# Row blocks of the normed x and the split weights at other addresses modulo 128

## What is computed

```
x = layer_norm(x, ln_emb_g, ln_emb_b)
h = x @ w_in + b_in                          # 1024 x 1992
...
x = layer_norm(DN_ALPHA * x + mix, ln1_g, ln1_b)
q = x @ xa_wq + bq
...
f = square(relu(x @ w_up + b_up)) @ w_down + b_down    # 1024 x 4096 and back
...
```

## Time and profile before

| what | value |
|---|---|
| median of three runs | 1988.37 us |
| the profiled execution's own time | 1989.87 us |
| its span, first to last instruction | 1988.1 us |
| granted TensorE clock, mean | 0.959 |
| TensorE (PE) busy | 1802.6 us, 91% |
| VectorE (DVE), ScalarE (ACT), GpSimd (POOL) busy | 967.8, 783.5 and 621.1 us |

### The profile page before, as it was taken

How to read it: one execution, slowest core, us unless ns; L and a number is a source line. 1 busy time by engine, 2 the same in 40 slices (tenths; PEclk the granted TensorE clock), 3 DMA queues, 4 the chain that set the end, 5 groups by cost and what they waited for, 6 DMA issues and landing times.

```text
span 1988.1 us, 22738 instructions
## 1 busy us (share of the span) xinstructions
PE 1802.6 (91%) x8994; PEld 1421.1 (71%) x8994; DVE 967.8 (49%) x1871; ACT 783.5 (39%) x1329; POOL 621.1 (31%) x223
## 2 busy tenths in 40 slices
PE   7895778989899999998988999999999899999998
PEld 6673554787788888887766777877787667676776
DVE  5167887444543121225646653455553544435355
ACT  4452453253264132313444444344445343433333
POOL 2332145121223434451233433443412132121320
PEclk9897889989999999998988999999999999999999
DMA  7212010121112222321111112221112111111101
GB/s 270 95 64 85 22 43 24 40 86 43 62 66 106 89 103 85 106 96 43 67 62 50 56 64 74 75 80 49 64 65 77 43 44 66 55 54 64 65 22 43
DMA packets 27409, 137.51 MB, mean 69 GB/s; under 512 B 2815, under 2 KB 9215, under 8 KB 13480
## 3 DMA queue, kind: packets, MB, share of 16 engines
q1 hardware_dynamic: 26248, 135.02, 19.2%
q10 hardware_dynamic: 1056, 1.05, 0.2%
HBM read 133.93 MB, written 2.12 MB: 68 GB/s over the span
## 4 chain that ended last, share of the span: by engine, by line
PE 68%; DVE 15%; ACT 9%; issue 4%; POOL 2%; DMA 1%; SPq 0%; DVEq 0%; ACTq 0%; POOLq 0%
PE ps L1166 67%; ACT whi L1564 2%; PE ps L1170 2%; POOL wlo L2502 1%; DVE STT L2414 1%; DVE XL L1996 1%; DVE tmp L2166 1%; DVE R L1996 1%; DVE mx L1999 1%; DVE SCB L2226 1%; ACT LG L1565 1%; DVE m L2224 1%; ACT tmp L1564 1%; ACT PM L1565 1%; ACT BH L1564 1%
## 5 line engine op out<-in xcount | busy, mean ns | idle before, releaser
L2502 POOL TENSOR_TENSOR wlo<-raw,whi 128x2048 fp32r<-128x2048 f32 (+3 forms) x123 | 527.2, 4286 | 1135.1 <-ACT whi L1564 1135.1
L1166 PE MATMUL ps<-XH,whi 128*128 128x512 f32 (+1 forms) x1144 | 447.8, 391 | 10.0 <-DVE XL L1996 4.7
L1166 PE MATMUL ps<-XH,wlo 128*128 128x512 f32 (+1 forms) x1144 | 425.9, 372 | 0.0
L1166 PE MATMUL ps<-XL,whi 128*128 128x512 f32 (+1 forms) x1144 | 425.9, 372 | 0.0
L1564 ACT ACTIVATE whi<-raw 128x2048 fp32r<-128x2048 f32 (+3 forms) x129 | 230.5, 1787 | 160.7 <-PE ps L1166 158.1
L1166 PEld LDWEIGHTS ps<-XH,whi 128*128 128x128 f32 x1144 | 221.6, 194 | 63.8 <-issue 20.0
L1166 PEld LDWEIGHTS ps<-XL,whi 128*128 128x128 f32 x1144 | 222.1, 194 | 36.5 <-issue 2.2
L1166 PEld LDWEIGHTS ps<-XH,wlo 128*128 128x128 f32 x1144 | 221.3, 193 | 37.5
L1166 PE MATMUL ps<-BH,whi 128*128 128x512 f32 (+1 forms) x608 | 229.1, 377 | 3.9 <-DVE BL L2436 2.0
L2096 DVE TENSOR_TENSOR R<-ps,R 128x512 f32<-128x512 f32 (+1 forms) x164 | 94.0, 573 | 270.3 <-PE ps L1166 269.9
L1166 PE MATMUL ps<-BH,wlo 128*128 128x512 f32 (+1 forms) x608 | 218.2, 359 | 0.0
(11 more groups left out here) (296 smaller groups left out, 2911.7 us busy)
## 6 DMA issues: line engine op xcount, KB each, us to landing
raw<-wall SPq DMA_DIRECT2D x108, 1024.0 KB, 4.6
raw<-wall SPq DMA_DIRECT2D x9, 512.0 KB, 3.3
raw<-wall SPq DMA_DIRECT2D x8, 576.0 KB, 3.4
raw<-wall SPq DMA_DIRECT2D x4, 768.0 KB, 4.0
R<-xT SPq DMA_DIRECT2D x1, 2048.0 KB, 13.9
BFL<-scr SPq DMA_DIRECT2D x16, 128.0 KB, 3.3
outT<-R SPq DMA_DIRECT2D x16, 128.0 KB, 1.9
MEM<-memT SPq DMA_DIRECT2D x2, 512.0 KB, 4.5
```

The source lines that it names most:

```text
L1166: return nc.tensor.matmul(o_, l, r_, start=start, stop=stop, skip_group_check=True)
L2502: tt(wlo[u % NSPL][:, 0:n], raw[u % NRAW][:, 0:n], f32(whi[u % NSPL][:, 0:n]), ALU.subtract).then_inc(S("g_lo"), 1)
```

## The change

It moves tiles; it adds and removes no instruction, and every engine has the same instructions, waits and order as before (12,626 instructions in both programs).

- The scratch for dynamic transfers at the bottom of each partition shrinks from 16384 to 128 bytes, and the counter starts at 512 and not at 16512. Both are multiples of 128.
- `whi0`, `wlo0`, `whi1`, `wlo1` now lie in this order with 32 bytes behind each: they start at 0, 32, 64 and 96 modulo 128.
- A row block of `XH` and `XL` now takes 516 elements (2064 bytes), of which 512 are used: row block k starts at 16 k modulo 128, in both tiles alike. `XL` starts 16512 bytes behind `XH`, again a multiple of 128.
- All other tiles keep their remainder modulo 128.

```diff
-        base = 16512
+        base = 512
...
         raw = [sb(f"raw{i}", [128, UNIT]) for i in range(NRAW)]
-        whi = [sb(f"whi{i}", [128, UNIT], F32R) for i in range(NSPL)]
-        wlo = [sb(f"wlo{i}", [128, UNIT], F32R) for i in range(NSPL)]
+        whi, wlo = [], []
+        for i in range(NSPL):
+            whi.append(sb(f"whi{i}", [128, UNIT], F32R))
+            top[0] += 32
+            wlo.append(sb(f"wlo{i}", [128, UNIT], F32R))
+            top[0] += 32
+        top[0] = (top[0] + 127) // 128 * 128
         x_at = top[0]
-        XH = sb("XH", [128, 8, T], F32R)
-        XL = sb("XL", [128, 8, T], F32R)
+        XH = sb("XH", [128, 8, T + 4], F32R)
+        XL = sb("XL", [128, 8, T + 4], F32R)
+        top[0] = (top[0] + 127) // 128 * 128
...
-                    return XH[:, k, :], XL[:, k, :]
+                    return XH[:, k, 0:T], XL[:, k, 0:T]
...
-    nc = _bacc.Bacc("TRN2", target_bir_lowering=False, num_devices=1)
+    nc = _bacc.Bacc("TRN2", target_bir_lowering=False, num_devices=1, dynamic_dma_scratch_size=128)
```

## The result

The changed kernel takes 1998.70 us (median of six runs, 1993.71 to 2003.88) against 1988.12 us before (six runs, 1987.53 to 1989.78): a ratio of 1.0052, with a 95% interval of 1.0031 to 1.0073. It is slower by half a per cent. Its six times fall in two groups of three, near 1993.8 and near 2003.7 us, so the median lies between them, where no execution is; the profiled execution, 2003.88 us, is of the upper one. The kernel before shows nothing like it in these six, but it does in later ones (see "The two groups of times").

A forecast was written before the change was run, and what follows sets the result against it. TensorE, busy 91% of the span, was taken as the bound through the spacing of its split matmuls. The terms summed to +5.7 us, nine tenths of it +5.1, so 1988.4 became 1993.5 us; 8-in-10 range 1972 to 2006.

The forecast's parts named there:

- a change of that spacing goes nearly straight into the time: Split matmuls on TensorE hardly wait, so their start spacing sets the time; nine tenths of a change reaches the end.
- the long stretch: 1344 matmuls in 306.40 us without TensorE idling; forecast about 308.7 us, under 303 if faster, over 312 if far slower.
- X, 512: 2664 matmuls on XH and XL, 512 columns: mean distance to the weights becomes the middle, 3.3 ns each, +8.8 us.
- B, 512: 1248 matmuls on BH and BL, 512 columns: even units +1.1 ns, odd units +5.5 ns, together +4.1 us.
- B2 and QC, 512: 600 matmuls on B2H, B2L, QCH, QCL, 512 columns: leave distance 64 for a mixture, -3.3 ns each, -2.0 us.
- X and B, 256: 1344 matmuls with 256 columns: spacing falls by half the gap between 120.1 and 113.4 ns, -4.5 us.
- B2, 256: 192 matmuls on B2H and B2L, 256 columns: spacing rises by 3.35 ns each, +0.6 us.
- a straight line between the two: Unread distances modulo 128 between 0 and 64 get interpolated spacings, 3.3 ns at distance 32; a choice, not a reading.
- B by unit: Sign: B's 512-column spacing should alternate, near 227.8 ns in even units and 232.2 ns in odd units.
- Nothing to measure: Rival: spacing settles near the old value or gains cancel losses; 1984.4 to 1992.4 us, chance 0.26.
- Faster: Rival: XH/XL 512-column matmuls drop 6.7 ns to 220 ns, 1972.4 us; with B, 1964.8 us; chance 0.30.
- Slower by far: Rival: settled pattern lost because starts shift with each row block; XH/XL, BH/BL at 233.3 ns, 2012.0 us, chance 0.10.

The follow-up runs named there:

- The kernels of constant distances: Kernel before with small scratch and counter at 512, weights or X, B, B2 moved to other fixed starts, no stagger: 1993.90, 1995.67, 2003.70 and 2000.78 us.

## Why the prediction was right, and where it was off

**The direction and the mechanism held.** The step "a change of that spacing goes nearly straight into the time" is borne out: the stretch without idle grew by 5.0 us and nothing hides it. The small scratch at 0 us was right, and GpSimd nearly so: TensorE waited 1.4 us longer at `wlo` before its largest group. The granted clock in the long stretch stayed at 1.00, as forecast.

The prediction also weighed the Trainium skill, page "TensorE: Matmul & The Clock Gate", section "Step-by-step: what each phase is for", by which the two read ports are independent and loading the next weights takes no read bandwidth from the running matmul. The reading put on it, that an address would then change nothing, is refuted: moving the weights alone took X from 226.7 to 232.3 ns. Whether that happens at the ports no run here shows.

**The size.** I forecast +5.1 us on the median; it is +10.6, just over twice that. How near that is to the sum below is in part luck, since the median lies between two groups: the lower is +5.7 us from the median before, the upper +15.7, and the ten later executions of the same kernel have a median of +7.6. That the lower group lies near the forecast is luck as well: its matmuls are spaced as in the upper, and its profiles lose 5 us less at the lower clock than that of the kernel before (table above). The spacings are the firmer measure. Averages over all steps at full clock that follow one another directly, before to after, against the terms of the sum:

| term | per matmul forecast | measured | us forecast | us measured |
|---|---|---|---|---|
| X, 512 | +3.3 ns | 227.9 to 231.6, +3.7 | +8.8 | +9.8 |
| B, 512 | +3.3 | 227.9 to 232.5, +4.6 | +4.1 | +5.8 |
| B2 and QC, 512 | -3.3 | 233.3 to 232.2, -1.1 | -2.0 | -0.7 |
| X and B, 256 | -3.3 | 119.7 to 117.8, -1.9 | -4.5 | -2.5 |
| B2, 256 | +3.35 | 114.8 to 117.8, +3.0 | +0.6 | +0.6 |

With the memory's keys (192 matmuls, -0.4; the 192 of the values are left out) the sum is +12.6 instead of +5.7. The step that was mis-sized is the choice "a straight line between the two" and, under it, the distance modulo 128. The line took every unread distance for the middle between a good and a bad reading; the measured function of the distance has one valley at 0, a shallow one at 64, and 232.4 to 234.3 everywhere else. So leaving 0 costs B 5.6 of the 6.7 ns in the long stretch, and leaving 192 (not 64, as the modulus turned out) for a mixture gains B2 little. The prediction took the distances of B's high weights in even units for 0; modulo 256 they are 128.

**Each sign.** The long stretch: forecast 308.7, measured 311.4, nearer to the "over 312" of the far case. B by unit: wrong in order, as shown. Modulo 256 the order comes out: even units have distances 128, 128 and 96, by the table 232.7 ns on average (measured 233.3), odd units 64, 64 and 32, by the table 230.4 (measured 231.3). X with 256 columns: fell, to 119.1 in the stretch shown and 117.9 on average, against "towards 117". The two groups of times were not foreseen; the range held both.

**The rivals.** "Nothing to measure" is out for the median (interval from 1.0031). "Faster" needs a spacing below 226.7 ns; none of the eight distances has one. "Slower by far", 2012 us, took all of X and B at 233.3 and no gain elsewhere. Its pattern is indeed lost: in the changed kernel B's steps in the long stretch range from 228 to 238 ns, where they were 226 or 227. But the reason it gave, a start that shifts with each row block, is not the cause: X at a constant distance of 32 takes 233.3 ns, and a shift of 256 costs nothing. Its price was twice too high, since the average over a staggered row is 231.5 and the settled 226.7 was itself reached only some matmuls after each wait (227.9 on average).

## What to carry to other kernels

For streams of split float32 products with 512 columns, keep the starts of moving operand and weights congruent modulo 256 bytes, row blocks and column slices included; then a gap or a row pitch is free. With 256 columns that rule did not hold here (below). When a tile order or a few odd-sized small tiles decide the remainder of a large operand, as they did for B2 here, one line of padding is worth trying: it gave 0.2% of this kernel. And before filling unread points with a line, measure one point between: the first one here (32 bytes) would have shown the bad plateau.

## What the runs showed of the hardware that I had not expected

- A matmul's spacing depends on where its moving operand starts relative to the weights: 226.7 to 234.3 ns for 512 columns, by the distance modulo 256 bytes, with the granted clock at 1.00 in all these windows. The kernels of constant distances have the same instructions in the same order. Whether its own weights count or the next ones, which are loaded meanwhile, and what in the chip makes the difference, no run here separates.
- With 256 columns the order is another: 120 ns at a distance of 0, but 113.4 ns for B2 at 192. The kernels of constant distances moved these groups too. Over all direct steps at full clock, X with 256 columns takes 119.7 ns at 0, 117.0 at 32, 116.7 at 64 and 118.3 at 224, B 119.8 at 96 and 118.2 at 160: 0 is among the slowest. No run gave 256-column groups a distance of their own, so what that would bring is not shown.
- The same program had executions 10 us apart with equal spacings, and 8.5 us of it lay in three stretches that differ in where the clock fell from 2.4 to 1.2 GHz: in dense matmuls or not. A comparison of the two kernels by single executions could have come out anywhere from no difference (1993.69 against 1994.07 us) to +0.8% (2003.88 against 1987.46).
